# Which pairs of an expert phase load their gate and up weights by contraction halves, and how the first unit's lead is cut

## What is computed

```python
gates = route(x, w_router, router_bias)             # top 8 of 64 experts for each token
hid = silu(x @ w_gate[e]) * (x @ w_up[e])           # w_gate, w_up: 64 x 1024 x 256
routed = sum over e of (hid * gates[e]) @ w_down[e]  # w_down: 64 x 256 x 1024
shared = (silu(x @ ws_gate) * (x @ ws_up)) @ ws_down
x = layer_norm(alpha * x + routed + shared, ln3_g, ln3_b)
```

## Time and profile before

| what | us |
|---|---|
| median of 3 runs | 1632.79 (1631.59 to 1633.2) |
| span of the profiled execution | 1629.2 |
| TensorE (PE) busy | 1585.8 (97%) |
| gate/up matmuls from units, line 1302 | 335.8 + 141.3 in 2032 |
| down matmuls, line 1343 | 168.1 + 65.8 in 1024 |
| VectorE busy | 384.1 (24%) |
| ScalarE busy | 304.2 (19%) |
| DMA | 509.96 MB, mean 313 GB/s |

### The profile page before, as it was taken

The page is one execution under the profiler, slowest core; times in us unless marked ns, Lnnn a source line. Parts: engine busy times, 40 slices in busy tenths (PEclk is TensorE's granted clock), DMA queues, the critical chain, the costliest instruction groups (busy, mean ns, idle before and its releaser), DMA issues.

```text
span 1629.2 us, 19711 instructions
## 1 busy us (share of the span) xinstructions
PE 1585.8 (97%) x7997; PEld 892.2 (55%) x7997; DVE 384.1 (24%) x827; ACT 304.2 (19%) x608; POOL 69.0 (4%) x88
## 2 busy tenths in 40 slices
PE   8999999999999999999999999999999999998995
PEld 7878868574344454333348788585733333333331
DVE  2222221052222211222221232212622111222213
ACT  1022011131222211112120230121422111211211
POOL 2000020020000000000020000201100000000000
PEclk9999999999999999999999999999999999999998
DMA  9246444459999999999992363416999999999996
GB/s 348 88 172 241 142 148 156 155 196 407 420 421 422 420 412 416 422 420 418 413 392 103 142 246 130 145 62 264 361 417 421 421 421 421 422 420 421 419 412 243
DMA packets 114604, 509.96 MB, mean 313 GB/s; under 512 B 8515, under 2 KB 16837, under 8 KB 72021
## 3 DMA queue, kind: packets, MB, share of 16 engines
q1 hardware_dynamic: 113952, 508.59, 78.2%
q0 software_dynamic: 224, 0.12, 0.0%
q10 hardware_dynamic: 340, 0.02, 0.0%
HBM read 507.64 MB, written 1.05 MB: 312 GB/s over the span
## 4 chain that ended last, share of the span: by engine, by line
PE 86%; SPq 6%; DMA 5%; DVE 2%; issue 1%; ACT 1%; DVEq 0%; ACTq 0%
PE work L841 40%; PE work L1302 23%; PE work L1343 11%; SPq L625 6%; DMA arena<-in_w_up 4%; PE moe_sum L1234 4%; PE work L1193 4%; PE moe_sum L1172 1%; PE work L1328 1%; DMA ring<-in_w_xk 1%; PE work L1200 0%; PE work L897 0%; PE work L1006 0%; PE work L1029 0%; PE work L1041 0%
## 5 line engine op out<-in xcount | busy, mean ns | idle before, releaser
L1302 PE MATMUL work<-ring,arena 128*64 128x512 f32 x1456 | 335.8, 593 | 4.9 <-DMA ring<-in_w_up 4.9
L841 PE MATMUL work<-XT,ring 128*128 128x256 f32 (+1 forms) x1408 | 280.5, 360 | 1.3 <-DVE arena L1885 1.3
L841 PEld LDWEIGHTS work<-XT,ring 128*128 128x128 f32 x1408 | 247.6, 190 | 32.6 <-issue 3.0
L1302 PEld LDWEIGHTS work<-ring,arena 128*64 128x64 f32 x1456 | 107.8, 137 | 209.1 <-issue 199.3
L1343 PE MATMUL work<-ring,hidden 128*64 128x512 f32 x736 | 168.1, 598 | 2.1 <-DVE hidden L2095 2.1
L1302 PE MATMUL work<-arena 128*64 128x512 f32 x576 | 141.3, 593 | 5.3 <-DMA arena<-in_w_up 5.3
L2102 DVE TENSOR_TENSOR out_lo<-work,out_hi 128x512 fp32r<-128x512 f32 x128 | 88.5, 692 | 230.6 <-ACT out_hi L1619 230.6
L841 PE MATMUL work<-ring,arena 128*128 128x512 f32 (+1 forms) x336 | 140.4, 577 | 0.0
L2091 DVE SCALAR_TENSOR_TENSOR hidden<-hidden,slot_gate,work 128x256 f32<-128x256 f32 x64 | 30.8, 481 | 409.5 <-ACT hidden L1613 409.5
L1619 ACT CAST out_hi<-work 128x512 fp32r<-128x512 f32 x128 | 75.0, 586 | 236.5 <-PE work L1343 236.5
L1613 ACT ACTIVATE hidden<-work 128x256 f32<-128x256 f32 x64 | 24.5, 383 | 420.9 <-PE work L1302 420.9
(11 more groups left out here) (230 smaller groups left out, 1271.2 us busy)
## 6 DMA issues: line engine op xcount, KB each, us to landing
ring<-in_w_down SPq DMA_DIRECT2D x92, 1024.0 KB, 17.4
ring<-in_w_gate SPq DMA_DIRECT2D x90, 1024.0 KB, 17.4
ring<-in_w_up SPq DMA_DIRECT2D x90, 1024.0 KB, 19.7
arena<-in_w_down SPq DMA_DIRECT2D x36, 1024.0 KB, 17.9
arena<-in_w_gate SPq DMA_DIRECT2D x36, 1024.0 KB, 17.0
arena<-in_w_up SPq DMA_DIRECT2D x36, 1024.0 KB, 19.7
ring<-in_w_in SPq DMA_DIRECT2D x28, 1024.0 KB, 13.4
ring<-in_w_mix_out SPq DMA_DIRECT2D x8, 1024.0 KB, 12.5
```

Of the source, the lines that this page charges most:

```text
L841: mm = pe.matmul(dst, a, b, start=(k == 0), stop=(k == len(pairs) - 1))
L1302: mm = pe.matmul(work[0][rows, :], gathered_pair(b, c, k)[:, rows], w, start=(c == 0), stop=(c == KC - 1))
```

## The change

The first body halves only pair 0 (before: pairs 0, 1, 2) and the last body only pair 7 (before: pairs 4 to 7). The constant LEAD goes. The lead now holds the first half of the contraction (chunks 0 to 3) of the pair's first expert, and the upper half of unit 0 the same of its second expert; both are loaded in one run of 4 KB per partition and DMA, where there were two runs of 2 KB. Sizes, places and the order of the loads stay as they are. TensorE waits for unit 0 together with the lead.

```diff
--- before.py
+++ after.py
@@ -50,7 +50,6 @@
 UNITS = 8
 LONG = UNITS + 1
 LONG_BODIES = 3
-LEAD = KC // 4
 LONG_ENDS = (26, 72)
 AHEAD_AT = 2
 AHEAD_UNITS = 2
@@ -265,7 +264,7 @@
 
         ahead = view(6 * K, UNITS - RING, SLOT)
         unit = [ring[:, u, :] if u < RING else ahead[:, u - RING, :] for u in range(UNITS)] + [arena[:, 0:SLOT]]
-        lead = lead_region[:, :].rearrange("p (w n) -> p w n", w=2)[:, :, 0:2 * LEAD * EXPERT_DIM]
+        lead = lead_region[:, :].rearrange("p (w n) -> p w n", w=2)[:, :, 0:KC // 2 * EXPERT_DIM]
         hid = hidden[:, 0:EXPERT_DIM]
         hidT = hidden[:, EXPERT_DIM:].rearrange("p (c s) -> p c s", c=2)
         gated = hidden[:, :].rearrange("p (k t) -> p k t", k=BATCH)
@@ -407,7 +406,7 @@
 
         def in_halves(q, j):
 
-            return q < 3 if j == 0 else q >= BATCH if j is None else False
+            return q == 0 if j == 0 else q == BODY_PAIRS - 1 if j is None else False
 
         def gathers_on(j):
 
@@ -608,9 +607,9 @@
                     for i in experts:
                         dst = unit[u][:, i * SLOT // 2:(i + 1) * SLOT // 2]
                         if m == 0 and j == 0:
-                            dst = unit[u][:, (2 + i) * SLOT // 4:(3 + i) * SLOT // 4].rearrange("p (e n) -> p e n", e=2)
-                            src = (e_gate, e_up)[i][bass.ds(pair_first, 2), :, LEAD:KC // 2, :
-                                                    ].rearrange("e p k f -> p e (k f)")
+                            dst = unit[u][:, (2 + i) * SLOT // 4:(3 + i) * SLOT // 4]
+                            src = (e_gate, e_up)[i][bass.ds(pair_first + 1, 1), :, 0:KC // 2, :
+                                                    ].rearrange("o p k f -> (o p) (k f)")
                         elif part == 2:
                             dst = dst.rearrange("p (k n) -> p k n", k=2)
                             src = e_down[bass.ds(pair_first + i, 1)].rearrange("o p k d -> (o p) k d")
@@ -631,8 +630,8 @@
                     alone(sp, x_split_ready, l * TT + 1)
                     alone(sp, seeded, l * TT + 1)
                     for i in range(2):
-                        sp.dma_start(lead[:, i, :].rearrange("p (e n) -> p e n", e=2),
-                                     (e_gate, e_up)[i][bass.ds(pair_first, 2), :, 0:LEAD, :].rearrange("e p k f -> p e (k f)")
+                        sp.dma_start(lead[:, i, :], (e_gate, e_up)[i][bass.ds(pair_first, 1), :, 0:KC // 2, :
+                                                                      ].rearrange("o p k f -> (o p) (k f)")
                                      ).then_inc(lead_loaded, 16)
 
                 first = [l * EXPERTS + 2 * q for q in range(BODY_PAIRS)]
@@ -1279,20 +1278,18 @@
                             pe.wait_ge(lead_loaded, (l + 1) * 32)
                         if 3 * q == LONG and j == 0:
                             pe.wait_ge(next_half_loaded, (l + 1) * 16)
-                        arrived = [] if leads else [wait_unit(3 * q + i) for i in range(1 if halves else 2)]
+                        arrived = [wait_unit(3 * q + i) for i in range(1 if halves else 2)]
                         for c in range(KC):
-                            if leads and c == LEAD:
-                                arrived.append(wait_unit(0))
                             if halves and c == KC // 2:
                                 arrived.append(wait_unit(3 * q + 1))
                             if k == 0:
                                 pe.wait_ge(gather_ready[c % 2], (batch + b) * (KC // 2) + (c // 2 + 1))
                             for e in range(2):
-                                if leads and c < LEAD:
-                                    w = lead.rearrange("p w (e k n) -> p w e k n", e=2, k=LEAD)[:, :, e, c, :]
+                                if leads and c < KC // 2 and e == 0:
+                                    w = lead.rearrange("p w (k n) -> p w k n", k=KC // 2)[:, :, c, :]
                                 elif leads and c < KC // 2:
-                                    w = arrived[0][:, SLOT // 2:].rearrange("p (w e k n) -> p w e k n", w=2, e=2, k=LEAD
-                                                                            )[:, :, e, c - LEAD, :]
+                                    w = arrived[0][:, SLOT // 2:].rearrange("p (w k n) -> p w k n", w=2, k=KC // 2
+                                                                            )[:, :, c, :]
                                 elif halves:
                                     w = arrived[c * 2 // KC].rearrange("p (w e k n) -> p w e k n", w=2, e=2, k=KC // 2
                                                                        )[:, :, e, c % (KC // 2), :]
```

## The result

The changed kernel takes 1637.78 us (median of 6 runs, 1636.35 to 1639.89) against 1632.87 us before (6 runs, 1631.59 to 1634.25): a ratio of **1.0032, 95% interval 1.0023 to 1.0042**, so 5 us slower. The forecast was 1633.3 with a range to 1636.8; both the time and "within 0.2%" were wrong.

The account below looks back on a forecast made before the run. The weight stream was taken to bound both expert phases. Layer 0 at +1.3 - 0.84 = +0.5 and layer 1 at +0.9 - 0.84 = +0.1 gave +0.5 us together, so 1633.3 us, range 1630.6 to 1636.8.

Parts of the forecast that it names:

- within 0.2%: Whole kernel: difference from before too small to tell, 0.2% or 3.3 us; chance put at 0.83.
- What bounds the phase: Expert phases: the weight stream sets each end, followed by one half contraction and what follows it.
- Edit 2, the run size: First body, pairs 1 and 2 whole: their weights are on hand, only the freeing moves; no run-size term.
- Edit 1, the end of the phases: Last body, pairs 4 to 6 whole: each saves 0.28 us of stream, -0.84 us a layer, at worst +0.14.
- The further 1.3 us: Last body: a whole pair's second unit lands 1.3 us earlier within the stream, so TensorE starts pair 6 sooner.
- that case: Phase ends without the 1.3 us: TensorE is last, +0.14 us in layer 1 and +0.12 in layer 0.
- Edit 2, units 12 and 15 late: Phase starts: unit 12 issued 3.43 us later costs +1.3 us in layer 0, +0.9 in layer 1; unit 15 nothing.
- the upper bound of 6.7: Phase start: unit 12's first DMA lands 4.7 to 6.7 us after its late issue, 5.7 taken.
- hole at the start: Rival: queue dry at unit 12's issue, whole 3.43 us lost in each layer, +5.2 us, 1638.0; chance 0.1.
- run size does nothing: Rival: 8 KB runs save no stream time, TensorE last at phase ends, about +2.6 us, 1635.4; chance 0.12.
- its rule that it is only worth it up to 256 bytes: Skill page's statement on merging descriptors into packets, cited with the no-run-size-effect rival as "would be this case"; no separate size.
- Edit 3: Lead and upper half of unit 0 in 4 KB runs: 0 us, bounds -0.1 to +0.1.

Follow-up runs that it names:

- e7: Kernel before, all runs still 4 KB, but SP waits for both halves of the first body's pairs 1 and 2 before loading units 12 and 15: 1636.01 us, 1.0017.
- the three comparisons: First body's pairs 1 and 2 whole with 8 KB runs (1.0037, 1.0031, 1.0034) set beside e7, e12 and e13 with 4 KB runs (1.0017, 1.0017, 1.0021).
- e2: Kernel before with only the last body's change, pairs 4 to 6 whole in 8 KB runs: 1632.70 us, 1.0005.
- e10: The same kernel as e2 run again, against the kernel before: 1631.71 us, 1.0003.
- e12: The same kernel as e7 run again, late freeing of pairs 1 and 2 alone, against the kernel before: 1635.67 us, 1.0017.
- e13: e7 plus TensorE waiting for both units of the first body's pairs 1 and 2, still 4 KB runs; against the kernel before 1635.94 us, 1.0021.
- e4: Kernel before, last body's pairs 4 to 6 waited for and freed as whole pairs but kept in 4 KB runs: 1637.19 us, 1.0025.
- e8: Kernel before with only the last body's pairs 4 and 5 made whole, 6 and 7 halved: 1632.59 us, 0.9999.

## Why the prediction was wrong, step by step

Two terms failed, each by 2 to 3 us: the gain at the end, which did not come, and the run size at the start, which had no term. The price of the late issue, on which the argument turned, came out about right as a sum.

- **What bounds the phase** (the stream, with TensorE's rest behind it): right. In layer 0 of the changed kernel the stream's shift at unit 13 (+3.2) came out at the phase's end (+3.7); e7 was 2.9 late at unit 13 and 1.6 at the end, so not every run keeps all of it.
- **Edit 2, the run size: a step that failed.** "Their own weights are on hand. What moves is the freeing": the sum has no term for the 8 KB runs of pairs 1 and 2. They cost 1.3 to 2.0 thousandths, 2.1 to 3.3 us, in the three comparisons, and a part of it can be seen before the delayed issue (330 to 350 GB/s from 380 to 388 us, where 4 KB runs have 388 and more).
- **Edit 1, the end of the phases: the other step that failed.** I forecast -0.84 us a layer, -1.7 in all; e2 and e10 have 1.0005 and 1.0003, +0.5 to +0.8 us. The run size's own saving came as forecast in layer 0: in e2, less its 0.43 us of offset, unit 19's up weights land at 807.4 where they landed at 808.2, 0.8 us earlier. The further 1.3 us, by which a whole pair's second unit was to land earlier within the stream, did not come. So TensorE is last, 16.1 us after unit 19, as the sum had said for that case (+0.14 and +0.12; e10 shows +0.2 and +0.2). The step that failed is that 1.3 us, taken from one whole pair before the last body and used for pairs 5 and 6 in it.
- **Edit 2, units 12 and 15 late: the sum was about right, its working was not.** I put +1.3 and +0.9 us on unit 12 and nothing on unit 15. Late freeing of both alone costs 2.8 us (e7, e12), whose interval, 1.3 to 4.2, includes 2.2. But no phase shows the forecast sizes: the stream was 0.0 to 2.9 us late at unit 13 in e7, e12 and e13. In layer 0 of the changed kernel the first DMA took 7.0 us from its issue, over the upper bound of 6.7, in layer 1 it took 5.0. The bounds came from two landings, and one number per layer can't stand for such a scatter. That the sum came close is luck in part.
- **The three together:** 2.8 + 2.1 to 3.3 + 0.5 to 0.8 = 5.4 to 6.9 us, against 5.2 (3.8 to 6.9) measured by the ratio of the changed kernel. The forecast was +0.5.
- **The rival "hole at the start"** gave 1638.0, and 1637.78 was measured. That is a coincidence of sums. Its price was 3.43 us of late issue in each layer, 6.9 together, less the gain of 1.7 at the end; late issue alone cost 2.8 us, the gain did not come, and the run size that makes up for it is not in it. Single phases do come close to its mechanism (2.9 in layer 0 of e7).
- **The rival "run size does nothing"** failed at both ends: between e4 and e2 the run size is worth 2.0 thousandths at the end of the phases, 3.3 us against a forecast 1.7, and at the start it costs. In the traces of e4 and e2 only 1.0 us of those 3.3 can be seen (shifts +2.5 and +0.8 against +0.2 and +2.1); each of them has one pair at the lower clock that reaches the end.
- **Beside this,** on the page "DMA: Bandwidth & Descriptors" of the Trainium skill, section "Why small descriptors are slow (HBM only)": its rule that it is only worth it up to 256 bytes is about putting consecutive descriptors into one packet. The prediction applied it to longer runs, of which it does not speak, and no run here tests the rule itself. 4 KB and 8 KB runs differ by 0.2% of the kernel's time at the end of the phases.
- **Edit 3** cost nothing, as forecast: 1.0002 (0.9993 to 1.0011).
- **TensorE's longer pairs.** I took 7 us for a pair's gate and up matmuls after any wait. After waits of 2.0 to 2.4 us it was 7.09 in some cases and 8.78 in others, the latter with a mean granted clock of 0.59 to 0.70 in the first 4 us (796.08 and 1474.15 in the changed kernel, 1483.51 in the earlier trace rows not). Pair 5 in layer 1 of the changed kernel, after 3.16 us, was hit too. In the changed kernel these fell on pairs with a later wait behind them, in e4 and e2 one each did not.
- **The scatter:** the profiled execution was 3.7 us below the median before (1632.87 - 1629.2) and is 3.2 below it after (1637.78 - 1634.6), so that the span's difference (5.4) is close to the medians' (4.9).

## What to carry to other kernels

Where a stream of loads bounds a phase, look for the moment when its queue is shortest. A later issue there can cost anything from nothing to its whole delay, from one phase to the next, so price it as a range and not as one landing. Two edits that a line of code makes together, here run size and freeing, need a term each, and a run each: both cost about as much. A gain that hangs on the order of landings needs its rows from the place where it is to be used. In this kernel freeing by halves paid at the start of a phase and waiting by halves at its end; making pairs 4 and 5 of the last body whole (e8) made no difference that can be told.

## What the runs showed of the hardware

- With the same DMAs in flight at nearly the same times, the stream moved 330 to 350 GB/s from 380 to 388 us in the five kernels whose pair 1 had been loaded in 8 KB runs, and 388 to 414 in the eleven others. Deep in the phase most slices of all of them have 420 to 422.
- A 1 MB DMA issued with little ahead of it landed 5.0 to 7.0 us after its issue (layers 1 and 0 of the changed kernel). Issuing it 3.43 us later made the stream between 0 and 3 us late two units on (e7, e12, e13).
- The two DMAs of a unit, issued half a us apart, land 2.5 us apart in some stretches and 5 us apart in others while the stream as a whole keeps its rate (around 740 us: 2.7 us in e13, 4.8 in e12, whose code differs in TensorE's waits only). So the wait for a unit can be over 2 us longer than the stream's position says. I did not find what sets it.
- Idling for about 2 us before a pair left TensorE's clock at its upper level in one place (1483.51 before, 7.09 us after 2.07 of idling) and took it to the lower one in another (1474.15 after, 8.78 us after 2.07 too), at 1.69 us for each pair hit.
